# A two-layer decoder trunk on one core: expert items gathered and turned for their own slots only

## The chip, the cores and the metric

The kernel runs on one core of a Trainium2 chip. The metric is the device time of one execution in microseconds (us). The kernel before takes 1507.82 us, the median of 3 runs (1506.71 to 1509.62). Device time includes everything from the first instruction to the last store of the output.

## What is computed

The program is two layers of a decoder trunk over 256 tokens of width 1024: a token mixer, a cross attention, and a channel mixer, with a final norm. The change lies in the channel mixer of the second layer, a mixture of eight experts of which each token uses two:

```
def moe_swiglu(h, w_router, wg, wu, wd):
    logits = (h @ w_router).astype(jnp.float32)
    top_v, top_i = lax.top_k(logits, TOP_K)
    gate = jax.nn.softmax(top_v, axis=-1)
    comb = jnp.sum(jax.nn.one_hot(top_i, N_EXPERTS, dtype=jnp.float32) * gate[..., None], axis=-2)
    out = jnp.zeros_like(h)
    for e in range(N_EXPERTS):
        out = out + comb[..., e:e + 1].astype(h.dtype) * swiglu(h, wg[e], wu[e], wd[e])
    return out
```

`swiglu(h, wg, wu, wd)` is `(silu(h @ wg) * (h @ wu)) @ wd`; wg and wu are 1024 x 3584, wd is 3584 x 1024, all in 32-bit floats. Each expert's weights are 42 MB, and all eight are read.

## The kernel before

**Items and steps.** The experts' work is cut into items. An item is one expert with up to 96 tokens (a large one, `CAP = 96`) or up to 64 (a small one, `SMALL_CAP = 64`). For this input there are eight: items 1, 4 and 7 are small (`SMALL_AT = (1, 4)` and the last), the others large. Each item has seven steps (`MOE_STEPS = 7`) of 512 hidden columns. A step needs three weight tiles of 2 MB: gate and up (`ring`, seven buffers in turn) and down (`down`, three buffers).

**Order on TensorE (PE).** `item` (L1486) issues for each step: the gate product into bank 0 and the up product into bank 1 (`up_e`, L1474 for a small item, L1479 and L1482 for a large one); then the down product of the step before (`down_e`, L1445 small, L1430 and L1434 large) into banks 2 and 3; then the turn of the step's hidden rows (`turn`, L1422). In the last step of an item, between the up product and the down product, `turn_rows(it + 1)` (L1411) turns the gathered tokens of the next item: eight transposes of 128 x 128 (L1414) from `xg` into banks 6 and 7. ScalarE (ACT) copies them to `e_in`, scaled by the norm's gain (L844), and the next item's up product reads `e_in` from there.

**The gather.** The normed tokens were stored to memory in `x_rows`. On GpSimd (POOL) `take(it)` (L449) waits until VectorE (DVE) has written the token numbers of the next item's slots (`take_next`, one number for each of 128 partitions, in step 4 of the item before) and issues an indirect DMA (L459) that reads one row of 4 KB for each of the 128 partitions of `xg`. Slots behind the item's own hold token numbers too, and their rows are read and turned, but no product reads them: `up_e` takes columns 0 to 95 of `e_in` in a large item and 0 to 63 in a small one. `put(it)` (L462) adds the finished rows of the item before to `sums` in memory by another indirect DMA (L472 for a large one, L469 for a small one).

**The weights' queue.** SyncE (SP) issues every weight load in one fixed order (`load_item`, L358; `load_up` L356, `load_down` L351): each waits until PE has used the tile that was in the buffer before (`w_used`).

**The end.** PE goes through the last item with a turn as well (`turn_rows(n_items)`), for an item that does not exist; POOL therefore has a last `take(n_items)` (L486). Behind it POOL loads `sums` into `x` (L494) when the last up product has been done (`w_used[1]`), and DVE adds the last item's rows (L2238), after a wait on the semaphore `xg_in` that counts the gathers and that load together.

Of the kernel before, what the change touches and what calls it, by code (L numbers as in the profile page):

```python
# [28 lines left out]
ACT = mybir.ActivationFunctionType  # L29
# [59 lines left out]
def build(nc, x_d, mem_d, wl_d, wf_d, wm_d, small_d, const_d, router_d, gfin_d, out_d):  # L89
    ctx = ExitStack()  # L90
    with ctx:
# [102 lines left out]
        def bank(i):  # L194
            return PS[:, i, :]
# [219 lines left out]
        @block.gpsimd  # L415
        def _(pool):
            pool.dma_start(small[:, 0:32], small_d[0, :, 0:32]).then_inc(gain_in, 16)
            pool.memset(stat[:, 2:4], -0.5).then_inc(consts_ready, 1)
            pool.memset(v_bd[:], 0.0).then_inc(consts_ready, 1)
            pool.wait_ge(consts_ready, 2)  # L420
            pool.wait_ge(second_in, 16)
            pool.dma_start(small[:, 32:SMALL_W], small_d[0, :, 32:SMALL_W]).then_inc(small_in, 16)

            def rstd(n):
                pool.wait_ge(ms_done, n)
                nc.gpsimd.tensor_tensor(stat[:, 6:8], stat[:, 4:6], stat[:, 2:4], ALU.pow).then_inc(rstd_done, 1)

            for l in range(DEPTH):
                for t in range(NT):
                    pool.wait_ge(m_ms, (1 if l == 0 else 4) + (t if l == 0 else 2 * t))  # L430
                    nc.gpsimd.tensor_tensor(rstd_mix[:, t:t + 1], stat[:, 4 + t:5 + t], stat[:, 2:3], ALU.pow).then_inc(m_rstd, 1)
                pool.dma_start(xs[:], mem_d.rearrange("(t p) d -> p t d", p=P)).then_inc(mem_in, 16)
                rstd(l * 2 + 1)
                pool.wait_ge(tq_done, l * 3 + 3)
                pool.memset(p_cmp[:], 0.0).then_inc(p_cmp_zero, 1)
                rstd(l * 2 + 2)
                for t in range(NT):
                    pool.wait_ge(f_ms, l * 4 + 2 * t + 2)
                    nc.gpsimd.tensor_tensor(stat[:, 6 + t:7 + t], stat[:, 4 + t:5 + t], stat[:, 2:3], ALU.pow).then_inc(f_rstd, 1)
                if l < DEPTH - 1:  # L440
                    pool.wait_ge(fn_hi, 4)
                    pool.wait_ge(fn_lo, 4)
                    pool.dma_start(small[:], small_d[l + 1]).then_inc(small_in, 16)
            pool.wait_ge(x_half, 8)
            pool.dma_start(sums[0:SEQ, :].rearrange("(t p) d -> p t d", p=P), x[:]).then_inc(put_done, 16)
            pool.wait_ge(fn_hi, 2 * NT + 2 * NT)
            pool.dma_start(x_rows.rearrange("(t p) d -> p t d", p=P), x_normed[:]).then_inc(put_done, 16)

            def take(it):  # L449
                pool.drain()  # L450
                pool.wait_ge(take_ready, it)
                if isinstance(it, int) and it == 1:
                    pool.wait_ge(put_done, 32)
                    pool.wait_ge(fn_lo, NT + 2 * NT)
                    pool.wait_ge(gath_done, 2)
                else:
                    pool.wait_ge(gath_done, it * 2)
                nc.gpsimd.tensor_tensor(pool_step[:], stat[:, 2:3], stat[:, 3:4], ALU.mult)
                pool.indirect_dma_start(out=xg[:], out_offset=None, in_=x_rows, in_offset=bass.IndirectOffsetOnAxis(ap=take_next[:], axis=0)) \  # L459
                    .then_inc(xg_in, 16)  # L460

            def put(it, small_before):  # L462
                pool.drain()
                pool.wait_ge(md_hi, it * 2)
                pool.wait_ge(put_ready, it)
                pool.wait_ge(put_done, it * 16 + 16)
                nc.gpsimd.tensor_tensor(pool_step[:], stat[:, 2:3], stat[:, 3:4], ALU.mult)
                if small_before:
                    pool.indirect_dma_start(out=sums.rearrange("r (h n) -> (r h) n", h=2), out_offset=bass.IndirectOffsetOnAxis(ap=put_now[:], axis=0),  # L469
                                            in_=down_rows[:, 0, :], in_offset=None, compute_op=ALU.add).then_inc(put_done, 16)  # L470
                else:
                    pool.indirect_dma_start(out=sums, out_offset=bass.IndirectOffsetOnAxis(ap=put_now[0:CAP, :], axis=0),  # L472
                                            in_=down_rows[0:CAP].rearrange("p b n -> p (b n)"), in_offset=None,
                                            compute_op=ALU.add).then_inc(put_done, 16)

            take(1)
            pool.wait_ge(items_ready, 1)
            pool.dma_start(gfin[:], gfin_d.partition_broadcast(P)).then_inc(gfin_in, 16)
            n_items = pool.value_load(items_i[0:1, NCOL:NCOL + 1], min_val=E, max_val=2 * E)
            for it in range(1, LAST_STATIC):  # L480
                put(it, it - 1 in SMALL_AT)
                take(it + 1)
            n_large = pool.value_load(items_i[0:1, NCOL + 1:NCOL + 2], min_val=E - N_SMALL, max_val=2 * E - N_SMALL)
            n_last = n_large + (N_SMALL - 1)
            with pool.Fori(LAST_STATIC, n_last) as it:
                put(it, False)  # L486
                take(it + 1)
            put(n_last, False)
            take(n_items)
            pool.drain()  # L490
            pool.wait_ge(put_done, n_items * 16 + 16)
            pool.wait_ge(w_used[1], n_items * MOE_STEPS + MOE_USED[1])
            nc.gpsimd.tensor_tensor(pool_step[:], stat[:, 2:3], stat[:, 3:4], ALU.mult)
            pool.dma_start(x[:], sums[0:SEQ, :].rearrange("(t p) d -> p t d", p=P)).then_inc(xg_in, 16)  # L494
            pool.wait_ge(gfin_in, 16)
            for t in range(NT):
                pool.wait_ge(x_half, DEPTH * 4 + t + 1)
                nc.gpsimd.tensor_tensor(part(xs[:, t, :], 0), part(x[:, t, :], 0), part(gfin[:], 0), ALU.mult).then_inc(xs_half, 1)
            pool.wait_ge(f_ms, DEPTH * 4 + 2)
            nc.gpsimd.tensor_tensor(stat[:, 6:8], stat[:, 4:6], stat[:, 2:4], ALU.pow).then_inc(f_rstd, 1)  # L500
# [3 lines left out]
        def _(act):  # L504
# [328 lines left out]
                nc.scalar.activation(a_T[:, 0:cols], bank(4)[:, 0:cols], ACT.Copy).then_inc(ma_done, 1)  # L833

            def item(it, small, small_before, n_read=None, n_moved=None, first=False):
                cols = QUART if small else HALF
                for s in range(MOE_STEPS):
                    n = it * MOE_STEPS + s
                    begin = first and s == 0
                    if s == 0:  # L840
                        for b in range(2):
                            act.wait_ge(gath_done, it * 2 + (b + 1))
                            for k in range(4 * b, 4 * b + 4):
                                ins = nc.scalar.activation(e_in[:, k, :], bank(6 + b)[:, (k % 4) * P:(k % 4) * P + P], ACT.Copy,  # L844
                                                           scale=sml("g_ffn", k, k + 1))
                            ins.then_inc(e_ready, 1)
                    if begin:
# [46 lines left out]
        def _(pe):  # L894
# [513 lines left out]
                    ins = mm(bank(5)[:, cols], f32(onehot[:, t, :]), info_tok[:, t, cols], start=(t == 0), stop=(t == NT - 1))  # L1408
                ins.then_inc(info_done, 1)

            def turn_rows(it):  # L1411
                pe.wait_ge(xg_in, it * 16)
                for k in range(KD):
                    ins = nc.tensor.transpose(bank(6 + k // 4)[:, (k % 4) * P:(k % 4) * P + P], xg[:, k * P:(k + 1) * P], ident)  # L1414
                    if k % 4 == 3:
                        ins.then_inc(gath_done, 1)

# [65 lines left out]
                                 start=(k == 0 and t == 0), stop=(k == KD - 1), skip_group_check=True)  # L1483
                ins.then_inc(w_used[kind], 1)

            def item(it, small, small_before, n_read=None, first=False):  # L1486
                for s in range(MOE_STEPS):
                    n = it * MOE_STEPS + s
                    begin = first and s == 0
# [2 lines left out]
                    if begin:  # L1492
                        pe.wait_ge(gt_ready, 1)
                        info(slice(0, 3))
                    if s == MOE_STEPS - 1:
                        turn_rows(it + 1)
                    if not begin:
                        if s == 1 and not first:
                            pe.wait_ge(md_hi, n_read)
# [35 lines left out]
                    last_rows(hf)  # L1535

            first_gather()
            item(0, False, False, first=True)
            for it in range(1, LAST_STATIC):
                item(it, it in SMALL_AT, it - 1 in SMALL_AT, it * 2 - 1)  # L1540
            pe.wait_ge(items_ready, 1)
            n_items = pe.value_load(items_i[0:1, NCOL:NCOL + 1], min_val=E, max_val=2 * E)
            with pe.If(n_items == E):
                item(LAST_STATIC, False, False, LAST_STATIC * 2 - 1)
                item(E - 1, True, False, E * 2 - 3)
                tail(E, E - 1)
            with pe.If(n_items > E):
                n_large = pe.value_load(items_i[0:1, NCOL + 1:NCOL + 2], min_val=E - N_SMALL, max_val=2 * E - N_SMALL)
                n_last = n_large + (N_SMALL - 1)
                with pe.Fori(LAST_STATIC, n_last) as it:  # L1550
                    item(it, False, False, it * 2 - 1)
                item(n_last, True, False, n_large * 2 + 3)
                tail(n_items, n_last)


# [1 line left out]
        def _(dve):  # L1557
# [681 lines left out]
                                           scalar=info_tok[:, t, 3:4], in1=part(x[:, t, :], hf),  # L2239
                                           op0=ALU.mult, op1=ALU.add).then_inc(x_half, 1)  # L2240

            dve.wait_ge(xg_in, n_items * 16 + 16)
            dve.wait_ge(oh_ready, n_items + 2)
            for hf in range(2):
                last_add(hf)
# [126 lines left out]
```

## Time and profile before

| what | value |
|---|---|
| median of 3 runs | 1507.82 us (1506.71 to 1509.62) |
| the profiled execution's own time | 1515.86 us |
| its span, first to last instruction | 1513.9 us |
| mean granted clock of TensorE | 0.983 |
| PE busy | 1462.7 us (97%) |
| DVE, ACT, POOL busy | 468.0, 387.7, 41.5 us |
| moved by DMA | 471.73 MB, mean 312 GB/s |
| transposes of gathered rows (L1414) | 64, in 8 groups |
| gathers (L459) | 8 |

Busy times are sums over the span; PE's busy time counts matmuls whose pipelined parts overlap. The span is what the views of the trace measure; the profiled execution is about 8 us longer than the median of the runs without a profile. The experts' part runs from about 645 us to the end of the span.

### The profile page before, as it was taken

The numbers are of one execution on the slowest core, as the hardware profiler recorded it, in microseconds if no ns is written. First come the engines' busy times: TensorE is split into PE (matmuls) and PEld (weight loads), VectorE is DVE, ScalarE is ACT, GpSimd is POOL, SyncE is SP. The second block draws the span as 40 slices with busy tenths as digits, with TensorE's granted clock in tenths as the row PEclk, the third lists the DMA queues.
The fourth block names the chain that finished last, engine by engine and source line by source line (L and its number), as shares of the span: only waits on it lengthen the run. The fifth ranks groups of instructions, "written<-read, shape, count | busy, mean of one in ns | idle before, by whom it ended". The sixth has DMA issues, their size and how long they took to land.

```text
span 1513.9 us, 39233 instructions
## 1 busy us (share of the span) xinstructions
PE 1462.7 (97%) x18070; PEld 1244.3 (82%) x18070; DVE 468.0 (31%) x752; ACT 387.7 (26%) x664; POOL 41.5 (3%) x63
## 2 busy tenths in 40 slices
PE   8999999999999999999998799999999799999996
PEld 7878888888897788899964599999865699999753
DVE  5767546666667575430000000000000000000002
ACT  6554434343556444220110100110111000100101
POOL 1000000000000000000000000000000000000001
PEclk9999999999999999999999899999999999999998
DMA  9424434455464344799999999999999999999995
GB/s 353 182 98 167 168 111 178 176 184 204 172 220 185 112 167 167 284 373 426 423 413 424 426 419 426 421 398 422 393 410 425 419 427 425 420 412 388 415 414 216
DMA packets 41274, 471.73 MB, mean 312 GB/s; under 512 B 4720, under 2 KB 6976, under 8 KB 11552
## 3 DMA queue, kind: packets, MB, share of 16 engines
q1 hardware_dynamic: 35664, 454.33, 73.6%
q0 software_dynamic: 3696, 13.31, 2.7%
q8 instruction: 139, 2.28, 0.6%
q10 hardware_dynamic: 1760, 1.68, 0.3%
q14 instruction: 15, 0.12, 0.0%
HBM read 463.18 MB, written 5.64 MB: 310 GB/s over the span
## 4 chain that ended last, share of the span: by engine, by line
PE 83%; DMA 14%; DVE 2%; ACT 1%; issue 0%; POOL 0%; POOLq 0%; SPq 0%; DVEq 0%; ACTq 0%
PE PS L1482 14%; DMA down<-wm_dram 12%; PE PS L1188 9%; PE PS L1479 9%; PE PS L1434 8%; PE PS L899 6%; PE PS L901 6%; PE PS L900 6%; PE PS L1430 5%; PE PS L1189 5%; PE PS L1474 4%; PE PS L1445 3%; PE PS L1422 1%; DMA w1v<-wl_dram 1%; PE PS L1250 1%; PE PS L1230 1%
## 5 line engine op out<-in xcount | busy, mean ns | idle before, releaser
L1482 PE MATMUL PS<-ring,e_in 128*32 128x128 f32 x3360 | 373.4, 273 | 0.0
L1479 PE MATMUL PS<-ring,e_in 128*32 128x384 f32 x3360 | 368.2, 487 | 0.0
L1482 PEld LDWEIGHTS PS<-ring,e_in 128*32 128x32 f32 x3360 | 364.0, 110 | 0.0
L2191 DVE TENSOR_TENSOR hid_tok<-PS,hid_tok 128x384 f32<-128x384 f32 (+1 forms) x56 | 28.4, 507 | 756.5 <-PE PS L1482 546.6
L1562 DVE TENSOR_TENSOR wlo<-stage,whi 128x2048 fp32r<-128x2048 f32 (+2 forms) x54 | 169.7, 3142 | 94.6 <-ACT whi L508 94.5
L1434 PE MATMUL PS<-down,a_T 128*32 128x128 f32 x1680 | 189.2, 273 | 0.0
L1430 PE MATMUL PS<-down,a_T 128*32 128x384 f32 x1680 | 186.9, 486 | 0.0
L1434 PEld LDWEIGHTS PS<-down,a_T 128*32 128x32 f32 x1680 | 183.0, 110 | 0.0
L1188 PE MATMUL PS<-pairB,whi 128*128 128x512 f32 x480 | 169.4, 397 | 1.7 <-DVE wlo L1562 1.2
L508 ACT ACTIVATE whi<-stage 128x2048 fp32r<-128x2048 f32 (+2 forms) x56 | 146.6, 2621 | 94.7 <-PE PS L901 52.3
L1474 PE MATMUL PS<-ring,e_in 128*32 128x256 f32 x2688 | 149.4, 380 | 0.0
L833 ACT ACTIVATE a_T<-PS 128x384 f32<-128x384 f32 (+1 forms) x56 | 25.1, 449 | 461.9 <-PE PS L1422 461.9
L1479 PEld LDWEIGHTS PS<-ring,e_in 128*32 128x32 f32 x3360 | 133.9, 109 | 4.9 <-issue 4.7
L1189 PE MATMUL PS<-pairB,wlo 128*128 128x256 f32 x480 | 134.7, 281 | 0.0
L1474 PEld LDWEIGHTS PS<-ring,e_in 128*32 128x32 f32 x2688 | 85.2, 110 | 57.1 <-issue 3.0
L1445 PE MATMUL PS<-down,a_T 128*32 128x256 f32 x1344 | 87.4, 418 | 31.2 <-DMA down<-wm_dram 30.8
L1188 PEld LDWEIGHTS PS<-pairB,whi 128*128 128x128 f32 x480 | 90.1, 188 | 23.8 <-DVE wlo L1562 1.5
L1445 PEld LDWEIGHTS PS<-down,a_T 128*32 128x32 f32 x1344 | 46.8, 120 | 68.4 <-DMA down<-wm_dram 33.7
L1189 PEld LDWEIGHTS PS<-pairB,wlo 128*128 128x128 f32 x480 | 90.7, 189 | 0.3
L861 ACT ACTIVATE hid_tok<-PS 128x384 f32<-128x384 f32 (+1 forms) x56 | 25.2, 450 | 218.7 <-PE PS L1482 163.2
L899 PE MATMUL PS<-whi,pairB 128*128 128x454 f32 (+1 forms) x192 | 73.3, 382 | 0.3 <-DVE pairB L1657 0.3
L901 PE MATMUL PS<-whi,pairB 128*128 128x454 f32 (+1 forms) x192 | 72.0, 375 | 0.0
(399 smaller groups left out, 1678.5 us busy)
## 6 DMA issues: line engine op xcount, KB each, us to landing
ring<-wm_dram SPq DMA_DIRECT2D x112, 2048.0 KB, 23.4
down<-wm_dram SPq DMA_DIRECT2D x56, 2048.0 KB, 23.9
stage<-wl_dram SPq DMA_DIRECT2D x20, 2048.0 KB, 7.8
stage<-wf_dram SPq DMA_DIRECT2D x33, 1024.0 KB, 4.7
stage<-wl_dram SPq DMA_DIRECT2D x4, 1816.0 KB, 8.5
w1k<-wl_dram SPq DMA_DIRECT2D x2, 2048.0 KB, 8.2
w1v<-wl_dram SPq DMA_DIRECT2D x2, 2048.0 KB, 8.3
third<-wl_dram SPq DMA_DIRECT2D x2, 1816.0 KB, 9.6
```

The source lines that it names most:

```text
L508: nc.scalar.activation(whi[slot][:, 0:n], (raw or stage[slot])[:, 0:n], ACT.Copy).then_inc(w_hi[slot], 1)
L899: mm(out, ah, bh, start=start, stop=False)
L901: return mm(out, al, bh, start=False, stop=stop)
L1188: mm(out, wh, pair[:, :, k, :], start=(k == 0), stop=False, skip_group_check=True)
L1189: return mm(out[:, 0, :], wl, pair[:, 0, k, :], start=False, stop=(k == KD - 1), skip_group_check=True)
L1430: mm(bank(2 + hf)[t * PIECE:(t + 1) * PIECE, 0:HALF], a, w[:, c, cols:cols + HALF], start=(start and c == 0), stop=(stop and c == 3), skip ...
L1434: ins = mm(bank(2 + hf)[CAP:P, t * P:(t + 1) * P], a, w[:, c, cols + HALF:cols + 512], start=(start and c == 0 and t == 0), stop=(stop and ...
L1445: ins = mm(bank(2 + q)[rows:rows + PIECE, 0:QUART], a_T[:, a0:a0 + PIECE], w[:, 2 * hh + c, d0:d0 + QUART], start=(start and i == 0), stop ...
L1474: ins = mm(bank(kind)[rows:rows + PIECE, 0:QUART], e_in[:, k, toks], w[:, k, h * QUART:(h + 1) * QUART], start=(k == 0), stop=(k == KD - 1 ...
L1479: mm(bank(kind)[rows, 0:3 * P], e_in[:, k, rows], w[:, k, 0:3 * P], start=(k == 0), stop=(k == KD - 1), skip_group_check=True)
L1482: ins = mm(bank(kind)[CAP:P, t * P:(t + 1) * P], e_in[:, k, t * PIECE:(t + 1) * PIECE], w[:, k, 3 * P:4 * P], start=(k == 0 and t == 0), s ...
L1562: V.tensor_tensor(wlo[slot][:, 0:n], (raw or stage[slot])[:, 0:n], f32(whi[slot][:, 0:n]), ALU.subtract).then_inc(w_lo[slot], 1)
```

## The change

`take` and `turn_rows` are told whether the item is small, and gather and turn 64 or 96 rows instead of 128. `turn_rows` transposes with the corner of the identity of that size, and ACT copies that many columns. The gather and the turn behind the last item are gone, and DVE's wait at the end counts one gather less.

```
@@ gpsimd
-            def take(it):
+            def take(it, small):
+                slots = SMALL_CAP if small else CAP
...
-                pool.indirect_dma_start(out=xg[:], out_offset=None, in_=x_rows, in_offset=bass.IndirectOffsetOnAxis(ap=take_next[:], axis=0)) \
+                pool.indirect_dma_start(out=xg[0:slots, :], out_offset=None, in_=x_rows,
+                                        in_offset=bass.IndirectOffsetOnAxis(ap=take_next[0:slots, :], axis=0)) \
...
-            take(1)
+            take(1, 1 in SMALL_AT)
...
             for it in range(1, LAST_STATIC):
                 put(it, it - 1 in SMALL_AT)
-                take(it + 1)
+                take(it + 1, it + 1 in SMALL_AT)
...
             with pool.Fori(LAST_STATIC, n_last) as it:
                 put(it, False)
-                take(it + 1)
+                take(it + 1, False)
             put(n_last, False)
-            take(n_items)
             pool.drain()
@@ scalar
-                                ins = nc.scalar.activation(e_in[:, k, :], bank(6 + b)[:, (k % 4) * P:(k % 4) * P + P], ACT.Copy,
+                                ins = nc.scalar.activation(e_in[:, k, 0:slots], bank(6 + b)[:, (k % 4) * P:(k % 4) * P + slots], ACT.Copy,
@@ tensor
-            def turn_rows(it):
+            def turn_rows(it, small):
+                slots = SMALL_CAP if small else CAP
                 pe.wait_ge(xg_in, it * 16)
                 for k in range(KD):
-                    ins = nc.tensor.transpose(bank(6 + k // 4)[:, (k % 4) * P:(k % 4) * P + P], xg[:, k * P:(k + 1) * P], ident)
+                    ins = nc.tensor.transpose(bank(6 + k // 4)[:, (k % 4) * P:(k % 4) * P + slots], xg[0:slots, k * P:(k + 1) * P],
+                                              ident[0:slots, 0:slots])
...
-                    if s == MOE_STEPS - 1:
-                        turn_rows(it + 1)
+                    if s == MOE_STEPS - 1 and not last:
+                        turn_rows(it + 1, small_next)
...
-                item(E - 1, True, False, E * 2 - 3)
+                item(E - 1, True, False, E * 2 - 3, last=True)
@@ vector
-            dve.wait_ge(xg_in, n_items * 16 + 16)
+            dve.wait_ge(xg_in, n_items * 16)
```

On PE the program of the last item's last step and the end before (`ring` and `down` are the weight tiles, `hid_tok` the step's hidden rows):

```order
L1474 MATMUL PS<-ring_136,e_in 32x256 x32
L1474 MATMUL PS<-ring_137,e_in 32x256 x32
L1414 MATMUL PS<-const,xg 128x128 x8
L1445 MATMUL PS<-down_101,a_T 32x256 x32
L1422 MATMUL PS<-const,hid_tok 128x128 x2
L1513 MATMUL PS<-const,onehot 128x128 x2
L1445 MATMUL PS<-down_100,a_T 32x256 x32
```

and with the change (its lines are three further down):

```order
L1477 MATMUL PS<-ring_136,e_in 32x256 x32
L1477 MATMUL PS<-ring_137,e_in 32x256 x32
L1448 MATMUL PS<-down_101,a_T 32x256 x32
L1425 MATMUL PS<-const,hid_tok 128x128 x2
L1516 MATMUL PS<-const,onehot 128x128 x2
L1448 MATMUL PS<-down_100,a_T 32x256 x32
```

The eight transposes between the last up product and the down product are gone; nothing else moved.

On POOL the end of the program before, from the last put on:

```order
L467 TENSOR_TENSOR pool_step<-stat 128x1
L472 DMA sums<-down_rows,put_now 384x1024
L457 REGISTER_ALU
L458 TENSOR_TENSOR pool_step<-stat 128x1
L459 DMA xg<-x_rows,take_next 128x1024
L491 ISA
L492 ISA
L493 TENSOR_TENSOR pool_step<-stat 128x1
L494 DMA x<-sums 128x2x1024
```

and with the change:

```order
L469 TENSOR_TENSOR pool_step<-stat 128x1
L474 DMA sums<-down_rows,put_now 384x1024
L492 ISA
L493 ISA
L494 TENSOR_TENSOR pool_step<-stat 128x1
L495 DMA x<-sums 128x2x1024
```

The last gather and its two steps ahead are gone. The other seven gathers stay where they were, 64 or 96 rows high.

## Rows read from the trace of the kernel before

**Rows 1.** The page: DMA rate over 40 slices; chain that ended last, by engine and line.

```profile
GB/s 353 182 98 167 168 111 178 176 184 204 172 220 185 112 167 167 284 373 426 423 413 424 426 419 426 421 398 422 393 410 425 419 427 425 420 412 388 415 414 216
...
PE 83%; DMA 14%; DVE 2%; ACT 1%; issue 0%; POOL 0%; POOLq 0%; SPq 0%; DVEq 0%; ACTq 0%
```

**Rows 2.** PE's waits inside the experts' part: start, us, instruction, [idle before <- releaser].

```profile
788.22 3.66 PE L1445 MATMUL PS<-down,a_T 128*32 128x256 f32 x64 [0.87 <-DMA down<-wm_dram]
...
866.45 6.57 PE L1445 MATMUL PS<-down,a_T 128*32 128x256 f32 x64 [11.19 <-DMA down<-wm_dram]
...
1168.39 5.35 PE L1445 MATMUL PS<-down,a_T 128*32 128x256 f32 x64 [3.47 <-DMA down<-wm_dram]
1192.87 5.51 PE L1445 MATMUL PS<-down,a_T 128*32 128x256 f32 x64 [8.14 <-DMA down<-wm_dram]
...
1480.11 5.25 PE L1445 MATMUL PS<-down,a_T 128*32 128x256 f32 x64 [2.38 <-DMA down<-wm_dram]
```

**Rows 3.** Stretches: engines' busy time (instructions), PE's granted clock, DMA share, GB/s.

```profile
672.00:866.00 194.00, 177.92 (x3082) 142.35 (x3073) 15.62 (x78) 17.50 (x45) 4.79 (x7) 0.96 1.01 423
873.00:1054.00 181.00, 181.00 (x3218) 177.10 (x3215) 9.49 (x33) 15.54 (x34) 5.83 (x8) 1.00 1.01 418
1054.00:1072.00 18.00, 18.00 (x318) 17.27 (x316) 0.56 (x1) 1.47 (x3) 0.00 (x0) 1.00 0.92 360
1072.00:1192.00 120.00, 108.95 (x1886) 76.21 (x1878) 5.71 (x20) 13.07 (x36) 2.86 (x4) 0.98 1.01 419
1198.00:1381.00 183.00, 183.00 (x3241) 178.43 (x3237) 9.58 (x33) 16.04 (x35) 5.85 (x8) 1.00 1.01 420
1381.00:1405.00 24.00, 24.00 (x438) 23.63 (x434) 0.56 (x1) 1.47 (x3) 0.00 (x0) 1.00 0.93 366
1405.00:1480.00 75.00, 72.73 (x1284) 47.87 (x1276) 4.82 (x18) 8.76 (x23) 2.86 (x4) 1.00 1.01 414
```

**Rows 4.** The chain that ended last, its end, in order of time: start, us, what.

```profile
1448.44 31.63 DMA down<-wm_dram
...
1492.77 1.02 PE PS L1414 x8
1493.80 3.59 PE PS L1445 x64
...
1502.74 0.76 DVE x L2238
```

**Rows 5.** The gathers: POOL's issues (count, ns, first and last start) and time to landing.

```profile
L459 POOL DMA_INDIRECT xg<-x_rows,take_next x8: 1003/1006/1067, 719.0 to 1469.0; - x8
...
DMA to landing us min/median/max: 11.3/11.8/12.5
```

**Rows 6.** Timeline of POOL: the gathers of items 2 and 5, the last gather, the last load.

```profile
812.12 1.02 POOL L459 DMA_INDIRECT xg<-x_rows,take_next  x1
...
1143.26 1.01 POOL L459 DMA_INDIRECT xg<-x_rows,take_next  x1
...
1469.05 1.00 POOL L459 DMA_INDIRECT xg<-x_rows,take_next  x1 [0.45 <-issue]
1492.90 0.18 POOL L493 TENSOR_TENSOR pool_step<-stat 128x1 f32<-128x1 f32 x1 [22.84 <-PE PS L1474]
1493.03 0.76 POOL L494 DMA_DIRECT2D x<-sums  x1
```

**Rows 7.** Stretches with a gather in flight, columns as in Rows 3.

```profile
719.00:731.00 12.00, 12.00 (x219) 11.63 (x210) 0.00 (x0) 0.98 (x2) 1.65 (x2) 1.00 1.01 423
...
1469.00:1481.00 12.00, 9.62 (x170) 5.21 (x162) 0.42 (x1) 0.77 (x2) 1.00 (x1) 0.96 1.02 431
```

**Rows 8.** Stretches around two waits of PE, columns as in Rows 3.

```profile
788.00:792.00 4.00, 3.78 (x66) 2.16 (x66) 0.00 (x0) 0.00 (x0) 0.27 (x1) 1.00 0.98 401
...
1480.00:1483.40 3.40, 3.29 (x32) 1.58 (x36) 0.00 (x0) 0.00 (x0) 0.00 (x0) 0.50 0.95 405
```

**Rows 9.** DMA queues' issues with KB and us to landing: the load of sums.

```profile
x<-sums POOLq DMA_DIRECT2D x1, 1024.0 KB, 5.2
```

**Rows 10.** ACT's copies of turned rows before item 1; columns as in Rows 2.

```profile
750.53 2.18 ACT L844 ACTIVATE e_in<-PS,small 128x128 f32<-128x128 f32 x8 [5.34 <-PE PS L1414]
```

**Rows 11.** The chain: the first product that reads those copies.

```profile
756.79 7.04 PE PS L1474 x128
```

More of the change, by code:

```diff
@@ L835, in item @@
             def item(it, small, small_before, n_read=None, n_moved=None, first=False):
-                cols = QUART if small else HALF
+                cols, slots = (QUART, SMALL_CAP) if small else (HALF, CAP)
                 for s in range(MOE_STEPS):
@@ L1484, in up_e, with item @@
                 ins.then_inc(w_used[kind], 1)
-            def item(it, small, small_before, n_read=None, first=False):
+            def item(it, small, small_before, n_read=None, first=False, small_next=False, last=False):
                 for s in range(MOE_STEPS):
@@ L1537, in _ @@
             first_gather()
-            item(0, False, False, first=True)
+            item(0, False, False, first=True, small_next=1 in SMALL_AT)
             for it in range(1, LAST_STATIC):
-                item(it, it in SMALL_AT, it - 1 in SMALL_AT, it * 2 - 1)
+                item(it, it in SMALL_AT, it - 1 in SMALL_AT, it * 2 - 1, small_next=it + 1 in SMALL_AT)
             pe.wait_ge(items_ready, 1)
@@ L1543, in _ @@
             with pe.If(n_items == E):
-                item(LAST_STATIC, False, False, LAST_STATIC * 2 - 1)
-                item(E - 1, True, False, E * 2 - 3)
+                item(LAST_STATIC, False, False, LAST_STATIC * 2 - 1, small_next=True)
+                item(E - 1, True, False, E * 2 - 3, last=True)
                 tail(E, E - 1)
@@ L1551, in _ @@
                     item(it, False, False, it * 2 - 1)
-                item(n_last, True, False, n_large * 2 + 3)
+                item(n_last, True, False, n_large * 2 + 3, last=True)
                 tail(n_items, n_last)
```

## The prediction

> **What bounds the kernel now.** I began with the page: in the experts' part, from about slice 18 on, DMA moves 373 to 427 GB/s, and the chain that ended last is 83% PE and 14% DMA [rows 1]. Neither bounds alone, so I looked for the places where they change over. PE waits for `down` loads in the small items only: the last and longest wait of item 1 ends at 866.45 us, that of item 4 at 1192.87, and item 7 has one, of 2.38 us, that ends at 1480.11 [rows 2]. In large items PE is busy in every microsecond. DMA, in turn, is at a share of 1.01 of its 16 engines nearly everywhere, and falls to 0.92 at 1054 to 1072 and to 0.93 at 1381 to 1405 [rows 3]: there all free buffers have been filled and the next load waits for PE. So the end is set by a chain of five pieces that hand over to each other: DMA until 866, PE through items 2 and 3 until about 1072, DMA until 1192.87, PE through items 5 and 6 until about 1405, DMA until 1480.11, and then PE to the last product [rows 2 to 4]. A saving counts only if it lies on the engine that holds the piece. The sum uses this rule throughout.
>
> **The price of a gathered row.** While a gather is in flight DMA moves 423 and 431 GB/s, as it does elsewhere (414 to 423 in the busy stretches) [rows 3, 7]. So a gathered byte takes the place of a byte of weights. At 423 GB/s the 128 rows of 4 KB (524288 bytes) cost 1.24 us of DMA; 64 rows fewer save 0.62 us, 32 fewer 0.31 us. That is the upper bound of a narrowed gather. The lower one is nothing: a 2 MB load has landed only when its slowest share has, the share in the rows is a mean over 16 engines, and no row tells whether the fullest of them gets fewer rows. I take the upper end, by the row nearest to it, the rate during gathers, and keep the lower one as a rival.
>
> **DMA pieces.** First piece, until 866.45: the gather for item 1 is issued at 719.0 [rows 5] and loses 64 rows, that for item 2 at 812.12 [rows 6] loses 32: 0.62 + 0.31 = 0.93 us. Third piece: the gather for item 4 lies in or just ahead of the lull of 1054 to 1072, where DMA waits for PE anyway: nothing (bounds 0 and 0.62). That for item 5, issued at 1143.26 [rows 6], loses 32 rows: 0.31 us. Fifth piece: the gather for item 7 is issued ahead of the lull of 1381 to 1405: nothing (bounds 0 and 0.62). Gathers for items 3 and 6 lie in PE's pieces and give nothing. The last gather, issued at 1469.05, disappears whole. Gathers take 11.3 to 12.5 us to land [rows 5], so it is still under way when PE's wait ends at 1480.11; I put nine tenths of its 1.24 us ahead of that load, 1.1 us (bounds 0 and 1.24). PE's wait there is 2.38 us long, so it can take 1.1 us, and even the upper bound of 1.86. DMA pieces in all: 0.93 + 0.31 + 1.1 = 2.34 us.
>
> **PE pieces.** Eight transposes take 1.02 us on the chain [rows 4]. The turns for items 3 and 6, at 96 columns, lie in PE's pieces. If time follows the columns each saves a quarter, 0.25 us; if the load of the 128 weight columns sets the pace, nothing. I take half, 0.13 us each: 0.26 us. The turns for items 1, 2, 4, 5 and 7 are followed by a wait of PE or a DMA piece: nothing, except that the one for item 7 might speed up the releases in the fifth piece (bounds 0 and 0.25). The turn behind the last item goes: 1.02 us, all on the chain, which runs from the last up product over this turn into the down product at 1493.80 [rows 4]. What could be late next is the load of `sums`, which is issued at 1493.03 and takes 5.2 us [rows 6, 9], so until 1498.2; DVE's add needs it at 1502.74 [rows 4], or 1501.72 with this term. That is covered by 3.5 us, and the add goes on waiting for PE.
>
> **What costs and gains nothing.** ACT's copies shrink from 128 to 96 or 64 columns; they start at 750.53, take 2.18 us [rows 10], and the product that reads them starts at 756.79 [rows 11], so they were covered by four microseconds of down product and stay covered. POOL's 1.0 us for the last gather's issue lies in front of a wait of 22.84 us for PE [rows 6]; nothing is queued behind it that could go earlier. DVE's wait at the end asks for one gather less; both gather and load had come long before.
>
> **The clock.** After a wait of 0.87 us, at 788.22, PE's granted clock stays at 1.00 and the 64 matmuls of L1445 take 3.66 us; after the wait of 2.38 us it is 0.50 (1.2 instead of 2.4 GHz) for 3.4 us, and they take 5.25 [rows 2, 8], against 3.59 at full clock [rows 4]: 1.66 us lost, on the chain. With 1.1 us taken off, the wait is 1.28 us long, between the two. Whether the clock then holds no row settles: I take 0 and keep 1.66 as the other end. The waits at 866.45 and 1192.87 stay many microseconds long, and go on losing the clock. A restart at another moment can make these two losses larger or smaller (6.57 and 5.51 us for the same 64 matmuls [rows 2]); I count that as 0, within 1.06 us either way.
>
> **Sum.** 2.34 + 0.26 + 1.02 = 3.6 us. The profiled execution's 1515.86 us becomes 1512.2. It is 8.0 us above the median of the runs; the same difference on the median gives 1507.8 - 3.6 = **1504.2 us**. The best end of all bounds is 3.6 + 1.66 (clock) + 0.62 (item 7's gather) + 0.62 (item 4's) + 0.25 (its turn) = 6.75 us, or 1501.1; the worst that leaves only the last turn's 1.02 gives 1506.8.
>
> **Rivals.**
> *The clock holds.* Everything as above, and the wait in item 7 gets too short for the clock to fall: 3.6 + 1.66 = 5.3 us, 1502.5. For it speaks the wait of 0.87 us that cost no clock, and 1.28 is nearer to that than to 2.38; against it, that the runs without a profile may not lose the clock there at all.
>
> *The fullest share stays as full.* Cutting slots from the top leaves some engines or ports with as many rows as before. Then narrowed gathers save nothing and only the last gather and turns count: 1.1 + 0.26 + 1.02 = 2.4 us, 1505.4, no change that could be told. For it speaks that a load waits for its slowest share; against it only the unchanged rate, which is a mean. The Trainium skill has a rule for this: its page "SBUF — State Buffer" ("Door 1: The DMA port swizzle") says that DMA bandwidth goes by how many of 16 ports the partitions reach, with partitions 0 to 63 on eight of them, eight partitions to each. By that rule 64 slots load each of these eight ports as 128 do, which is this rival; no run so far shows shares of single ports.
>
> *The pieces are longer than they look.* If a saving in DMA only lengthens the next lull, as in the lulls above, the last turn alone remains: 1.02 us, 1506.8. Against it speak the shares of 1.01 through the first, third and fifth piece [rows 3].
>
> *Slower: the rows bunch up.* If an indirect DMA of 64 or 96 rows is dealt to fewer engines than one of 128, each of those carries more. With 128 rows on 16 engines each has 8, worth the 1.24 us above. On four engines 64 rows make 16 each and 96 rows 24, which is 2.5 and 3.7 us instead of 1.24, on the three gathers that lie in DMA pieces: 1.2 + 2.5 + 2.5 = 6.2 us lost against 2.4 gained, or 1511.6. It decides from about 13 rows on one engine, where the three extra delays of 0.8 us eat up the gain. Nothing in the rows shows it; the gathers' landing times would.
>
> **How the numbers follow.** About 3 us, 0.2%, can be told from no change here. Forecast and near it: 0.34, of which 0.04 lies under 3 us. The clock holds: 0.28. The fullest share: 0.26. Savings lost in lulls: 0.07. Bunched rows: 0.05. Faster by over 0.2% is 0.30 + 0.28 = 0.58; within 0.2% is 0.04 + 0.26 + 0.07 = 0.37; slower 0.05. The range takes in all but the last and reaches from the best to the worst bound, 1501.0 to 1506.8.
>
> **What would show it.** In the profile after: 7 gathers and 56 transposes; the down product directly behind the last up product; the waits that ended at 866.45 and 1192.87 ending about 0.9 and 1.4 us earlier (0 and 0.1 if the fullest share holds); PE's wait in item 7 near 1.3 us; the granted clock behind it 0.50 or 1.00; about 1.8 MB less moved. Wrong would be a wait that still ends at the same time, a lull that grows by what was saved, or a gather that takes longer to land than 12.5 us.

## The result and the profile after

The changed kernel is slower: 1515.93 us, the median of 7 runs (1513.79 to 1518.77), against 1510.19 us for 7 runs of the kernel before taken with it (1506.71 to 1513.91). The ratio is 1.0042, with a 95% interval of 1.0029 to 1.0055: 4 to 8 us lost, where 3.6 us of gain were forecast. Ratios, here and below, leave out two executions far off all others, 4402.4 us in one kernel of experiment 8 and 1844.87 us in the kernel before beside it. The two profiled executions hide this, with spans of 1513.9 before and 1513.7 after: the one of before, at 1515.86 us, took longer than any of its seven timed runs, and the one of after, at 1515.51, is one of its seven. So the traces are compared by their pieces, not by their ends.

The page of the profile after, total, DMA rate over 40 slices and the two largest queues (packets, MB, share of 16 engines' span):

```profile
span 1513.7 us, 39213 instructions
...
GB/s 352 174 107 172 162 111 179 188 176 211 161 230 175 112 173 161 315 378 427 410 410 410 427 419 409 425 410 403 402 412 410 419 425 408 406 411 389 418 413 219
...
DMA packets 40842, 470.03 MB, mean 311 GB/s; under 512 B 4704, under 2 KB 6960, under 8 KB 11120
...
q1 hardware_dynamic: 35664, 454.33, 74.2%
q0 software_dynamic: 3264, 11.61, 2.6%
```

and the same two queues before:

```profile
q1 hardware_dynamic: 35664, 454.33, 73.6%
q0 software_dynamic: 3696, 13.31, 2.7%
```

1.7 MB less is moved, as the change says. But queue q1, which carries the weights, moves the same 35664 packets and 454.33 MB in 74.2% of the span instead of 73.6%: 0.6% of 1514 us, so 9 us more of all 16 engines (8.1 us if the packets' times are added up). The slices that stood at 423, 413 and 424 [rows 1] stand at 410. The transfers have become slower, not more.

Where, the stretches behind the gathers tell: in the kernel after, seven microseconds each, from about four behind the issue of the gathers for items 1, 2, 3 and 5 (columns as in Rows 3; the last two are DMA share and GB/s):

```profile
720.00:727.00 7.00, 7.00 (x132) 6.94 (x134) 0.00 (x0) 0.98 (x2) 0.00 (x0) 1.00 1.01 351
814.00:821.00 7.00, 5.06 (x96) 2.78 (x88) 0.42 (x1) 0.39 (x1) 0.00 (x0) 1.00 1.01 341
936.00:943.00 7.00, 7.00 (x131) 7.00 (x134) 0.00 (x0) 0.98 (x2) 0.00 (x0) 1.00 1.01 334
1143.00:1150.00 7.00, 5.64 (x108) 3.12 (x96) 0.42 (x1) 0.39 (x1) 0.00 (x0) 1.00 1.02 344
```

and before, at the same places behind the issues:

```profile
723.00:730.00 7.00, 7.00 (x131) 7.00 (x133) 0.00 (x0) 0.98 (x2) 0.00 (x0) 1.00 1.02 424
816.00:823.00 7.00, 5.37 (x100) 2.99 (x92) 0.42 (x1) 0.38 (x1) 0.00 (x0) 1.00 1.02 428
939.00:946.00 7.00, 7.00 (x131) 6.89 (x133) 0.00 (x0) 0.98 (x2) 0.00 (x0) 1.00 0.99 413
1147.00:1154.00 7.00, 6.69 (x128) 3.81 (x124) 0.42 (x1) 0.39 (x1) 0.00 (x0) 1.00 1.01 426
```

The share is 0.99 to 1.02 before and 1.01 to 1.02 after, so the engines are as busy; the rate falls by about 80 GB/s. In seven microseconds that is 0.56 MB not moved, 1.3 us at 425 GB/s, for a gather that saves 0.13 or 0.26 MB, 0.3 or 0.6 us.

A lower rate alone does not show slower weights. In the kernel before it falls nearly as far behind `put`, which stores 96 rows (issued at 1119.37, columns as above):

```profile
1122.00:1129.00 7.00, 7.00 (x130) 4.07 (x126) 0.00 (x0) 0.77 (x2) 0.00 (x0) 1.00 1.02 367
```

The single packets, which the trace has and the views only sum up, tell the two apart. Behind that `put` the 16 KB packets of the weight loads take 622 ns on average, as elsewhere (614 to 620 in the four stretches of before), and the `put`'s own 4 KB packets take 328 ns, twice the 162 ns of a gather's. In the four stretches of after it is the weights' packets that take longer, 750 to 782 ns.

PE's waits for `down` loads after, to be held against [rows 2]:

```profile
785.91 3.66 PE L1448 MATMUL PS<-down,a_T 128*32 128x256 f32 x64 [1.77 <-DMA down<-wm_dram]
...
864.93 4.95 PE L1448 MATMUL PS<-down,a_T 128*32 128x256 f32 x64 [11.36 <-DMA down<-wm_dram]
...
1193.41 6.24 PE L1448 MATMUL PS<-down,a_T 128*32 128x256 f32 x64 [9.82 <-DMA down<-wm_dram]
...
1480.94 5.35 PE L1448 MATMUL PS<-down,a_T 128*32 128x256 f32 x64 [2.52 <-DMA down<-wm_dram]
```

The end of the chain after has lost its transposes: the down product stands directly behind the last up product.

```profile
1486.65 7.04 PE PS L1477 x128
1493.70 3.45 PE PS L1448 x64
```

So the part of the change at the end did what it says, and the narrowed gathers, meant to relieve the transfers, hold them up.

### The profile page after: what moved, and what is told of

It reads as the page before. It is cut to its first block, busy times and chain, and to the rows that moved or that the text cites. A ratio compares the mean times of both kernels' runs of the same rounds, so it can differ in the third digit from the quotient of the medians.

```text
span 1513.7 us, 39213 instructions
## 1 busy us (share of the span) xinstructions
PE 1454.0 (96%) x18062; PEld 1238.4 (82%) x18062; DVE 467.8 (31%) x752; ACT 385.5 (25%) x664; POOL 39.9 (3%) x61
## 3 DMA queue, kind: packets, MB, share of 16 engines
q1 hardware_dynamic: 35664, 454.33, 74.2%
## 4 chain that ended last, share of the span: by engine, by line
PE 83%; DMA 14%; DVE 2%; ACT 1%; issue 0%; POOL 0%; SPq 0%; POOLq 0%; DVEq 0%; ACTq 0%
PE PS L1485 14%; DMA down<-wm_dram 12%; PE PS L1189 9%; PE PS L1482 9%; PE PS L1437 8%; PE PS L900 6%; PE PS L902 6%; PE PS L901 6%; PE PS L1433 5%; PE PS L1190 5%; PE PS L1477 4%; PE PS L1448 4%; PE PS L1425 1%; DMA w1v<-wl_dram 1%; PE PS L1251 1%; PE PS L1231 1%
## 5 line engine op out<-in xcount | busy, mean ns | idle before, releaser
L900 PE MATMUL PS<-whi,pairB 128*128 128x454 f32 (+1 forms) x192 | 73.6, 383 | 0.3 <-DVE pairB L1660 0.3
L901 PE MATMUL PS<-wlo,pairB 128*128 128x454 f32 (+1 forms) x192 | 72.1, 376 | 0.0
```

The source lines that it names most:

```text
L900: mm(out, ah, bh, start=start, stop=False)
L901: mm(out, ah, bl, start=False, stop=False)
```

## The experiments

Two theories stood at the start. **A:** a narrowed gather slows the weight loads beside it; the rest of the change is good. **B:** the loss comes from the end, where the last gather and turn are gone. Each ratio below is against the kernel before, run beside it on the same chip.

**1. Only the last gather and turn removed.** All other gathers and turns stay 128 high.

```
             put(n_last, False)
-            take(n_items)
...
-                    if s == MOE_STEPS - 1:
+                    if s == MOE_STEPS - 1 and not last:
                         turn_rows(it + 1)
```

> The kernel before without the gather and the turn behind the last item; all other gathers and turns 128 high. Theory A (a narrowed gather slows the weight loads beside it, and the rest of the change is good): no narrowed gather is left, so the gain of the last gather and turn shows alone, 2.1 us or 0.1% faster than before, up to 3.8 us if the clock holds in item 7; DMA moves over 410 GB/s during each gather. Theory B (the loss comes from the end of the program, where the last gather and turn are gone): slower than before by about 6 us, as the whole change is.

Measured: 1507.84 us against 1511.64, ratio 0.9975 (0.9963 to 0.9987). B falls: this part gains, 2 to 6 us, at the upper end of what A gave it. The last wait of this kernel's PE shows why:

```profile
1475.82 3.66 PE L1444 MATMUL PS<-down,a_T 128*32 128x256 f32 x64 [0.23 <-DMA down<-wm_dram]
```

The wait in item 7 has shrunk from 2.38 to 0.23 us, and the 64 matmuls behind it take 3.66 us, not 5.25: the clock held.

**2. Only the gathers narrowed.** The tokens' rows in slots behind an item's own are not fetched, and the last gather takes 96 rows; all eight turns stay 128 high.

```
-                pool.indirect_dma_start(out=xg[:], out_offset=None, in_=x_rows, in_offset=bass.IndirectOffsetOnAxis(ap=take_next[:], axis=0)) \
+                pool.indirect_dma_start(out=xg[0:slots, :], out_offset=None, in_=x_rows,
+                                        in_offset=bass.IndirectOffsetOnAxis(ap=take_next[0:slots, :], axis=0)) \
```

> The kernel before with the gathers for items 1 to 7 narrowed to 64 or 96 rows, and nothing else; all eight turns stay 128 high, and turn whatever lay in the other rows of the tile, which no product reads; the last gather takes 96 rows. Theory A: slower than before by 6 to 10 us (the whole change lost 6.3, of which about 2 us were a gain by the last gather and turn); DMA falls to 300 to 380 GB/s for some 6 us behind each gather. Theory B, or a rival by which narrowed turns are slow: within 2 us of before. By bytes alone: 1 us faster.

Measured: 1520.36 us against 1511.64, ratio 1.0058 (1.0040 to 1.0076), 8.7 us slower. The whole loss, and more, is in the gathers. The stretch behind the gather for item 2, four microseconds behind its issue:

```profile
813.00:820.00 7.00, 5.69 (x108) 3.16 (x100) 0.42 (x1) 0.38 (x1) 0.00 (x0) 1.00 1.02 330
```

**3. As many rows and bytes as before, as two gathers of 64.** The second takes the tokens of the first 64 slots again, into partitions 64 to 127.

```
+                for h in range(2):
+                    rows = slice(h * 64, (h + 1) * 64)
+                    pool.indirect_dma_start(out=xg[rows, :], out_offset=None, in_=x_rows,
+                                            in_offset=bass.IndirectOffsetOnAxis(ap=take_next[0:64, :], axis=0)) \
+                        .then_inc(xg_in, 16)
```

> The kernel before with each gather of 128 rows made as two of 64 rows, partitions 0 to 63 and 64 to 127; the second takes the tokens of the first 64 slots again, so the output differs from the reference. As many rows and bytes as before. Theory A in the form that the way rows are dealt to the engines matters, not their number: slower than before by 8 to 20 us, with the weights' rate down during both halves. Rival, that one half of the partitions is overloaded when the other gets nothing: both halves are filled here, so within 2 us of before, at most 1 us slower per gather for the second issue.

Measured: 1532.10 us, ratio 1.0136 (1.0118 to 1.0153), 20.5 us slower, with no byte more and both halves of the partitions filled. Neither the number of rows nor a neglected half makes the loss. What 16 gathers instead of eight cost by themselves is in this time too; the kernels of experiments 4 and 6 have no second gather.

```profile
816.00:823.00 7.00, 5.63 (x108) 3.12 (x96) 0.42 (x1) 0.38 (x1) 0.00 (x0) 1.00 1.01 313
```

**4. The bytes of a 64-row gather in all 128 partitions.** Experiment 1 with gathers of 128 half rows of 2 KB.

```
-                pool.indirect_dma_start(out=xg[:], out_offset=None, in_=x_rows, in_offset=bass.IndirectOffsetOnAxis(ap=take_next[:], axis=0)) \
+                pool.indirect_dma_start(out=xg[:, 0:512], out_offset=None, in_=x_rows.rearrange("r (h n) -> (r h) n", h=2),
+                                        in_offset=bass.IndirectOffsetOnAxis(ap=take_next[:], axis=0)) \
```

> Without the last gather and turn, and each gather takes 128 rows of 2 KB instead of 4 KB, so that it moves the bytes of a 64-row gather into all 128 partitions; half of each token's row is left out, so the output differs from the reference. Theory A: DMA keeps over 410 GB/s during gathers, and the time is that of the kernel without the last gather and turn, less up to 1.9 us for three halved gathers in DMA-bound pieces: 2 to 4 us faster than before. Rival, that any smaller gather slows the weights (its packets come in a different rhythm): slower than before, as with narrowed gathers.

Measured: 1505.50 us, ratio 0.9957 (0.9941 to 0.9973), 6.1 us faster than before. Fewer bytes cost nothing if all 128 partitions take part. They seem to gain: the ratio's interval overlaps that of experiment 1, but from the last wait of item 1 to that of item 4 the trace has 324.2 us, against 326.4 there. The rate stays where it was:

```profile
819.00:826.00 7.00, 7.00 (x136) 4.24 (x132) 0.42 (x1) 0.38 (x1) 0.00 (x0) 1.00 1.01 426
```

**5. The changed kernel with its gathers wide again.** Turns and copies stay narrow.

```
-                pool.indirect_dma_start(out=xg[0:slots, :], out_offset=None, in_=x_rows,
-                                        in_offset=bass.IndirectOffsetOnAxis(ap=take_next[0:slots, :], axis=0)) \
+                pool.indirect_dma_start(out=xg[:], out_offset=None, in_=x_rows,
+                                        in_offset=bass.IndirectOffsetOnAxis(ap=take_next[:], axis=0)) \
```

> The changed kernel with its gathers widened to 128 rows again; turns and copies stay at 64 or 96, and nothing is gathered or turned behind the last item. Theory A: the loss is gone, and it runs as the kernel that only drops the last gather and turn, 0.2 to 0.4% faster than before, at most 0.3 us better than that one for the narrower turns of items 3 and 6; DMA moves over 410 GB/s during gathers. If narrowed turns cost something themselves, it is slower than the kernel that only drops the last ones.

Measured: 1508.63 us against 1510.45, ratio 0.9988 (0.9979 to 0.9997). The loss is gone, and the rate is back (behind the gather for item 2). The interval overlaps that of experiment 1, so a gain or cost of the narrowed turns can't be told at this size.

```profile
817.00:824.00 7.00, 7.00 (x136) 4.25 (x132) 0.42 (x1) 0.38 (x1) 0.00 (x0) 1.00 1.02 430
```

**6. 112 rows.** Experiment 1 with gathers of 112 rows, which is seven times 16.

```
-                pool.indirect_dma_start(out=xg[:], out_offset=None, in_=x_rows, in_offset=bass.IndirectOffsetOnAxis(ap=take_next[:], axis=0)) \
+                pool.indirect_dma_start(out=xg[0:112, :], out_offset=None, in_=x_rows,
+                                        in_offset=bass.IndirectOffsetOnAxis(ap=take_next[0:112, :], axis=0)) \
```

> Without the last gather and turn, each gather takes 112 rows of 4 KB, partitions 0 to 111 (the turns stay 128 high). Theory A1, that any number but 128 is dealt to the engines so that they write where other engines' weights go: slower than the kernel that only drops the last gather and turn by 6 to 12 us, with the rate down to 300 to 380 GB/s behind gathers. Theory A2, that the imbalance between the upper and the lower 64 partitions makes the loss (64 of 64 and 48 of 64 here, against 32 at 96 rows): slower by less than 4 us.

Measured: 1520.59 us, ratio 1.0060 (1.0045 to 1.0075): 10 us slower than before, and by the two ratios some 13 slower than experiment 1, for an eighth of the rows left out. The upper half of the partitions is three quarters full here, and the loss is no smaller; it is a little over what form A1 allowed. A1 holds, A2 falls.

```profile
816.00:823.00 7.00, 4.95 (x92) 2.73 (x84) 0.42 (x1) 0.38 (x1) 0.00 (x0) 1.00 1.04 341
```

**7. Is it the indirect DMA?** Experiment 1 with each gather replaced by a plain DMA of rows 0 to 63, and in a second kernel of rows 0 to 127.

```
-                pool.indirect_dma_start(out=xg[:], out_offset=None, in_=x_rows, in_offset=bass.IndirectOffsetOnAxis(ap=take_next[:], axis=0)) \
-                    .then_inc(xg_in, 16)
+                pool.dma_start(xg[0:64, :], x_rows[0:64, :]).then_inc(xg_in, 16)
```

> Without the last gather and turn; each gather is replaced by a plain DMA of rows 0 to 63 of the normed tokens into 64 partitions, 4 KB each, issued at the same place on GpSimd. The tokens are the wrong ones, so the output differs from the reference. If the loss comes from how any transfer of fewer than 128 rows is dealt to the engines: 5 to 10 us slower than the kernel with plain transfers of 128 rows. If it belongs to the indirect DMA: as that kernel, less the bytes saved, within 2 us.

> As the kernel with plain transfers of 64 rows, but of rows 0 to 127 into 128 partitions; the output differs from the reference for the same reason. Both theories: as the kernel that only drops the last gather and turn, 0.1 to 0.3% faster than before, with DMA over 410 GB/s during these transfers.

Measured: 1513.98 us with 64 rows, ratio 1.0017 (1.0006 to 1.0029), and 1507.45 with 128, ratio 0.9976 (0.9967 to 0.9986). Half the bytes cost 6.5 us. So it is no property of the gather: a plain transfer of 64 rows does it as well. Behind the transfer for item 2 the first kernel has

```profile
816.00:823.00 7.00, 5.93 (x112) 3.30 (x104) 0.42 (x1) 0.38 (x1) 0.00 (x0) 1.00 1.03 358
```

and the second

```profile
812.00:819.00 7.00, 5.82 (x108) 3.25 (x100) 0.42 (x1) 0.38 (x1) 0.00 (x0) 1.00 1.01 424
```

**8. Does the place matter?** Experiment 1 with narrowed gathers for items 3 and 6 alone (in PE's pieces by the prediction's rule), and in a second kernel for items 1, 2 and 5 alone (in DMA's pieces).

```
+                slots = (SMALL_CAP if it in SMALL_AT else CAP) if isinstance(it, int) and it in (3, 6) else P
+                pool.indirect_dma_start(out=xg[0:slots, :], out_offset=None, in_=x_rows,
+                                        in_offset=bass.IndirectOffsetOnAxis(ap=take_next[0:slots, :], axis=0)) \
```

> Without the last gather and turn; of the gathers only those for items 3 and 6 are narrowed, to 96 rows; they lie in the stretches in which PE is never idle. Theory A with the chain of pieces (a slower transfer costs only where the transfers hold the chain): each costs the transfers about 2 us, and the lulls that follow can take 1.5 us each, so 0 to 2 us slower than the kernel that only drops the last gather and turn, and still no slower than before. Rival, that every narrowed gather costs its full time: 3.5 to 4 us slower than that kernel.

> Without the last gather and turn; the gathers for items 1, 2 and 5 alone are narrowed, to 64, 96 and 96 rows; they lie in the pieces of the chain that the transfers hold. Theory A with the chain of pieces: each costs 1.5 to 2.5 us, all on the chain: 4.5 to 7.5 us slower than the kernel that only drops the last gather and turn, 1 to 4 us slower than before. If every narrowed gather costs the same wherever it lies, it is three sevenths of the 10 us by which narrowing all costs, 4 us, and items 3 and 6 cost 3 us in their kernel.

Measured: 1510.48 us with items 3 and 6, ratio 0.9999 (0.9987 to 1.0011); 1511.08 with items 1, 2 and 5, ratio 1.0001 (0.9992 to 1.0011). Against experiment 1's 0.9975 these are 3.6 and 3.9 us lost. The second is less than the pieces allowed, the first more; both lie near what an equal cost for every narrowed gather gives. These two ran on another occasion than experiment 1, so the medians alone would not decide. The traces help. This table has the ends of PE's last wait in item 1, in item 4 and in item 7, and what lies between:

| kernel (narrowed gathers issued in between) | item 1 | item 4 | item 7 | 1 to 4 | 4 to 7 |
|---|---|---|---|---|---|
| before (none) | 866.45 | 1192.87 | 1480.11 | 326.4 | 287.2 |
| experiment 1 (none) | 863.66 | 1190.03 | 1475.82 | 326.4 | 285.8 |
| items 3 and 6 alone (3; 6) | 864.76 | 1192.09 | 1479.00 | 327.3 | 286.9 |
| items 1, 2 and 5 alone (5; none) | 862.96 | 1190.30 | 1475.92 | 327.3 | 285.6 |
| all (3, 4, 5; 6, 7) | 864.93 | 1193.41 | 1480.94 | 328.5 | 287.5 |

Against experiment 1, item 3's gather in PE's piece costs 1.0 us, as much as item 5's in DMA's; item 6's costs 1.1, and without a narrowed gather the last column stays at 285.6. These are single profiles. Two more kernels without narrowed gathers, that of experiment 5 and the one with plain transfers of 128 rows, have 326.3 and 325.8 us from item 1 to item 4, and 286.5 and 286.4 from item 4 to item 7. So 0.9 to 1.5 us for items 3 and 5 stand clear; item 6's may be as little as 0.4. The lull took up only a part of what came late. In 40 us around it the DMA share is 0.96 in experiment 1 (the first row) and 0.97 with item 3's gather narrowed (the second); 7 GB/s more are 0.28 MB, or 0.7 us, and still item 4's wait ended 1.0 us later:

```profile
1036.00:1076.00 40.00, 40.00 (x723) 39.27 (x719) 1.68 (x6) 2.46 (x5) 1.18 (x2) 1.00 0.96 390
```

```profile
1038.00:1078.00 40.00, 40.00 (x724) 39.27 (x719) 1.68 (x6) 2.46 (x5) 1.18 (x2) 1.00 0.97 397
```

**9. A kernel that fetches less without narrowing.** The small items 1 and 4 need 64 rows; here their gathers take 128 half rows, partition p the first half of slot p's token and partition 64 + p the second, and four transposes turn both halves. The rest is as in experiment 5.

```
+                halves = it in SMALL_AT if isinstance(it, int) else False
+                rows = x_rows.rearrange("r (h n) -> (r h) n", h=2) if halves else x_rows
+                pool.indirect_dma_start(out=xg[:, 0:D // 2 if halves else D], out_offset=None, in_=rows,
+                                        in_offset=bass.IndirectOffsetOnAxis(ap=take_next[:], axis=0)) \
...
+                            V.tensor_tensor(take_next[:], info_next[:, 2:3], upper[:], ALU.add).then_inc(take_ready, 1)
```

> The changed kernel with gathers of 128 rows, and for the small items 1 and 4 these are 128 half rows of 2 KB: partition p takes the first half of slot p's token, partition 64 + p the second half; four transposes then turn both halves. Same result as the reference. Theory A: as the kernel with wide gathers and narrow turns, less 0.6 us for item 1's gather and up to 0.6 us for item 4's, so 0.25 to 0.45% faster than before; the fastest of these kernels, by less than a run can tell.

Measured: 1507.09 us against 1510.45, ratio 0.9973 (0.9963 to 0.9983). With experiment 1 it beats both kernels of this case; which of the two is faster can't be told.

**All kernels together.** The weights' queue q1 moves 35664 packets and 454.33 MB in each of them. Its share times the span, each within 0.8 us, is 1113 to 1115 us in the six kernels with no transfer narrowed (before, experiments 1, 4, 5 and 9, and the one of 128 rows in 7). It is 1117 us in the two with two or three narrowed ones, 1121 to 1123 with seven or eight, and 1131 with sixteen of 64 rows. That is 1 to 1.5 us of all 16 engines for each, wherever it lies.

## Why the prediction was wrong

**The step that failed** is the price of a gathered row: "a gathered byte takes the place of a byte of weights". From an unchanged rate during gathers of 128 rows I concluded that a smaller gather costs in proportion, 0 to 0.62 us saved. That holds if 128 partitions take part (experiment 4). With 64, 96 or 112 rows a gather costs more than one with 128: by the table about 1 us each on the chain, and by the rate 80 GB/s less for seven microseconds. The lower bound of nothing was no bound, for no row excluded a loss, and every gather in the trace had the same 128 rows, so none could show one. The puts of 96 rows, which read from the partitions, left the weights' packets as they were.

**DMA pieces.** Forecast 0.93 us gained until item 1's last wait. Against the issue of the store of `x_rows` that stands ahead of the items, 648.57 us before and 645.64 after,

```profile
645.64 0.72 POOL L447 DMA_DIRECT2D x_rows<-x_normed  x1 [10.06 <-ACT x_normed L791]
```

the wait ended 1.4 us later (219.3 against 217.9). That measure is not firm. Counted from the first load of the experts' weights on SP's queue (597.86 before, 595.16 after) it is 1.2 us; by this count the kernels with wide gathers for items 1 and 2 lie between 267.5 and 268.6 us, after at 269.8, and the kernel with items 1, 2 and 5 narrowed at 268.5. So the gain did not come, but how much this piece lost is open. For item 5's gather, 0.31 us were forecast to be gained; its kernel lost about 1.0. Item 7's gather was counted at 64 rows, but the changed `take(it + 1, False)` fetches 96 for it, so 1.7 MB less is moved and not 1.8; of the sum only a bound hung on it.

**The rule of the pieces** did not hold, as far as single profiles show. A slower transfer in PE's pieces was not free, and cheaper ones gained there too. In experiment 4 item 1 to item 4 is 1.7 to 2.3 us shorter than in the kernels with wide gathers, near the 1.9 us that three halved gathers (items 3, 4 and 5) are worth by the bytes; by the rule item 5's 0.6 alone would count. The lulls are not the full slack that I took them for; why late loads still cost while DMA's share falls there stays open.

**The last gather and turn.** Forecast 1.1 + 1.02 us, with 1.66 more if the clock held: 3.8. Experiment 1 gives 3.8 (2.0 to 5.6), and experiment 5, which has the same end, 1.8 (0.5 to 3.2). The turn is gone from the chain, and item 4 to item 7 is 1.4 us shorter by the table. The wait, forecast at 1.28 us, is 0.23 and 1.26 us in these two, and the clock held in both. In the changed kernel the wait stayed at 2.52 us and the clock fell, 5.35 us for the 64 matmuls. So this term was right in its mechanism, and the rival "the clock holds" too, but not in the changed kernel. That the length of the wait decides is not shown: in the kernel with items 3 and 6 narrowed, 3.44 us ahead of the product at 1152.69 cost no clock (3.66 us for the 64 matmuls), and 2.24 us in item 7 did (5.22).

**Narrow turns.** 0.13 us each was forecast for items 3 and 6. The eight transposes of 96 columns take 0.81 instead of 1.02 us on the chain, and those of 64 columns 0.64:

```profile
963.00 0.81 PE PS L1416 x8
```

so the time goes down with the columns, by 0.21 us for 96. The load of `sums`, ACT's copies and POOL's end cost nothing, as forecast.

**The rivals.** "The fullest share stays as full" saw that rows cut from the top might not help, but priced it at nothing gained; experiment 6 shows that the top half is not the point. "The rows bunch up" had the sign, and by luck nearly the size for the whole change (6.2 us lost on three gathers), but not the mechanism. In the changed kernel gathers landed in 9.4 to 11.8 us, sooner than before, so no engine carried a long tail. Those of 112 rows did take 11.7 to 13.4 us, past the 12.5 that was named as a sign. But rows bunched on a few engines would hold up the weights of these few, and nearly all packets of the weights took longer, as the next paragraph has it.

**The cause.** Shown: a gather of 64, 96 or 112 rows of 4 KB, and a plain transfer of 64, slows the 128-row weight loads in flight; the bytes of 64 rows in 128 partitions don't. From five to eight microseconds behind the issue, outside the lulls, nearly every 16 KB packet of the weights takes longer. In each of these microseconds it is 735 to 981 ns on average beside the narrowed transfers of all kernels here, and 611 to 640 beside those into 128 partitions. The second kernel of experiment 8 has both: 749 to 866 ns beside the gathers for items 1, 2 and 5, and 615 to 626 beside those for items 3 and 6. With 64 rows this lasts some five microseconds, with 96 seven, with 112 up to eight, which fits the larger loss of experiment 6. Not shown is what collides, since no view here tells the engines apart. The Trainium skill has what fits. Its page "DMA: Bandwidth & Descriptors" says under "The descriptor swizzle" that in a transfer to 128 partitions each engine writes the eight partitions of one port of its own; under "Why a DMA increments its semaphore by 16 and not by 1", that a transfer is split over the largest number of engines up to 16 that divides the outer count of both its sides, here the rows, which is 16 for 64, 96 and 112 alike. Worked out from the two, eight rows for each engine match the ports and six, four or seven don't, so engines would write where others' weights arrive; "Back-pressure in remote DMA", told of transfers between cores, says that a saturated port of the destination clogs the path back to the engines. All measured signs agree with that, experiments 3, 4 and 6 above all, and the puts, which read from the partitions and leave the weights' packets as they were; no run here shows single engines or ports.

## What to carry to other kernels

Where loads of 128 partitions keep the DMA engines full, a small transfer into the partitions beside them should have 128 partitions too: rows that nobody reads were cheaper than leaving them out, by about 1 us for each transfer. To move fewer bytes, make the rows shorter, not fewer. And a cost that is read from rows of one shape bounds nothing for another shape: a row for 128 partitions gave neither the size nor the sign of the cost at 96.

## What the runs showed of the hardware that was not expected

- Seven transfers of 64 to 96 rows cost the weights' queue 8 to 9 us of all 16 engines, with the same packets and bytes (73.6% of 1513.9 us against 74.2% of 1513.7).
- Leaving out 16 of 128 rows cost no less than leaving out 64 or 32: 341 GB/s behind the gather for item 2 with 112 rows and with 96 in the changed kernel, 428 with 128.
- The engines' busy share does not show it: 1.01 to 1.04 at 341 GB/s, 1.02 at 428. The rate has to be read beside the share, and where a rate falls, the time of the single packets tells whose transfer became slower.
- A transfer of 96 rows out of the partitions (`put`) did not slow the weight loads: 622 ns for their 16 KB packets beside it, 750 to 782 beside gathers of 64 and 96 rows into them.
